# Gates and branch projections of a hybrid layer moved to token order, 512 columns wide, with the merged sum turned on TensorE

## The chip, the cores and the metric

One core of one Trainium2 chip. The metric is the device time of one execution in microseconds (us), the median of several runs. TensorE is called PE, VectorE DVE, ScalarE ACT, GpSimd POOL, SyncE SP.

## What is computed

Two blocks of two layers each, on 256 tokens of width 1024 in float32. Only a layer of the first block is touched:

```
x = x + 0.5 * swiglu(rms_norm(x, ffn1_norm), ...)
z = rms_norm(x, mix_norm) @ w_in                    # u, q, k, v (512 each), gl (2048)
y_pool = multiscale_pool(u, pool_w, pool_scale)     # [tokens, 512]
y_attn = moba_attention(rope(norm(q)), rope(norm(k)), v)
gates  = sigmoid(gl + b_gate).reshape(B, S, 2, D)
merged = gates[:, :, 0] * (y_pool @ w_branch_pool) + gates[:, :, 1] * (y_attn @ w_branch_attn)
x = x + merged @ w_out
x = x + 0.5 * swiglu(rms_norm(x, ffn2_norm), ...)
```

With 256 tokens in one block of keys the attention is causal softmax attention of 8 heads of 64. The second block has a mixer of its own (neighbourhood attention and retention, m = 0 to 41) that has token order already.

## The kernel before

Every product with a weight is made of three matmuls in a reduced float32 form (upper x lower, lower x upper, upper x upper parts; `product`, L1603 to L1606). The weights come as a stream of chunks of 128 x 2048 (1 MB) through SP's queue into three slots. For each chunk ACT makes the upper part (L562), DVE the lower part (L1007), PE uses both. Step m of an engine's program begins with a wait for PE to have finished chunk m (`chunk_done`), and ends with the split of the chunk that comes into the same slot, m + 3 (`split_after`). PE takes chunk m when its lower part is there (`take`).

There are two forms of product. `features` (L1643) holds 128 x 128 of the weights still and streams 256 tokens: the result has features on the partitions, two tiles of 256 columns in one PSUM bank, 48 matmuls for a chunk. `wide_tokens` (L1683) and `wide_whole` (L1700) hold 128 tokens of the activation still and stream 512 columns of weights: the result has tokens on the partitions, one bank for each half of the tokens (a = 0, 1), 24 matmuls for a chunk. `wide_tokens` takes the inner dimension in two chunks (part 0 and 1); it is used for v (m = 4, 5), for the output (m = 20 to 23) and in the second block.

The mixer of the first block runs over 24 chunks, m = 0 to 23: q and k (0 to 3), v (4, 5), u (6, 7), gate 0 (8 to 11), gate 1 (12 to 15), pool branch (16, 17), attention branch (18, 19), output (20 to 23). The order of every engine is written out by hand, step by step:

- PE, L1895 to L1964. Gate chunks 8 to 15 go by `features` to bank 4 or 5 by the parity of m; before chunk m PE waits for `mix_scaled` m - 7, the evacuation of chunk m - 2. Behind the chunk of a step come the pool product (m = 10), the weighing of the values (`weigh_values`, L1832, even m from 10), the transposes of the softmax weights (`turn_weights`, L1816, m = 8 to 15) and the scores (L1801, odd m from 7 to 13). The branches go by `features` to banks 0, 1 (m = 16), 2, 3 (17), 4, 5 (18) and 2, 3 (19). The product with the output weights wants the merged sum with features on the partitions, in upper and lower parts; chunks 20 and 21 wait for these (`merged_lo`).
- DVE, L1208 to L1290. Step m: wait for chunk m; evacuate the bank of a gate (times the norm's factors of the tokens, L1233, m = 6 to 15); the maxima of the scores of head m - 7 (L1149, L1157); the lower part of an attention pair (L1022, even m); the softmax weights (L1168), which wait for ACT's exponentials; the split (L1007), which waits for ACT's. At m = 16 and 17 the gate is multiplied by the pool branch; at m = 18 come four rounds of multiply and add for the attention branch and the lower parts of the sum (L1268 to L1286).
- ACT, L733 to L813. Step m: copies of turned weights (L679), exponentials (L660), the upper part of the split (L562), and at m = 15 and 16 the sigmoids of a gate, 8 instructions of 256 columns with the bias as a column (L803). At m = 18 the upper parts of the sum (L689).
- POOL, L473 to L504, the reciprocal roots of the heads' norms (L475) and the pool branch's sums (L481 to L503), which start when u has been evacuated (m = 7).

The second block turns its merged sum already: `turn_merged` (L1983) transposes tiles of 128 x 128 on PE into banks 6 and 7, ACT takes upper parts from there (L851), DVE lower ones.

## Time and profile before

| | |
|---|---|
| median of 3 runs | 1969.69 us (1969.32 to 1970.82) |
| the profiled execution | 1969.46 us |
| its span, first to last instruction | 1967.6 us |
| PE busy | 1955.9 us, 99% |
| DVE, ACT, POOL busy | 1363.1, 1029.6, 160.4 us |
| mean granted clock of PE | 0.999 of full speed |
| HBM | 182 GB/s over the span |
| chain that ended last | PE 98%, DVE 1%, ACT 1% |

Matmuls overlap: a busy time counts each from its start to its modelled end, so the price of a stretch of PE is read from the start of its first instruction to the start of the next one behind it. In the timeline a row is: start, duration, engine, line, operation, output and inputs, array and shape, count, and in brackets the idle time before it and what ended it. PE, DVE and ACT work at the same time; idle time of DVE or ACT costs something only where PE then waits.

### The profile page before, as it was taken

What the parts mean: (1) busy time and instruction counts of PE and PEld (TensorE: products, weight loads), DVE (VectorE), ACT (ScalarE), POOL (GpSimd) and SP (SyncE); (2) the same over time, 40 slices, a digit from 0 to 9 for tenths busy, and PEclk for the clock granted to TensorE, in tenths of its full rate; (3) what the DMA queues carried; (4) which work ended last, traced back from release to release, by engine and by line L of the source; (5) the groups of instructions that cost most, each with busy time, mean ns of one, the idle gap of its engine ahead of it and who ended that gap; (6) DMA issues with size and microseconds to landing.
All of it is one profiled execution on the core that took longest, in us unless ns stands there. A gap on an engine that the chain in (4) does not pass through costs nothing.

```text
span 1967.6 us, 28691 instructions
## 1 busy us (share of the span) xinstructions
PE 1955.9 (99%) x11078; PEld 1691.2 (86%) x11078; DVE 1363.1 (69%) x1660; ACT 1029.6 (52%) x1209; POOL 160.4 (8%) x148
## 2 busy tenths in 40 slices
PE   9999999999999999999999999999999999999998
PEld 8888999888888889998888978888888978888887
DVE  7666577666676666667666566577888666677887
ACT  6444545544454454565444553456556554456564
POOL 0000130000000003103001201040001301000000
PEclk9999999999999999999999999999999999999999
DMA  8555544555455545446555544564553554555552
GB/s 326 192 185 178 185 154 176 175 189 192 171 193 192 184 161 190 150 173 230 190 192 174 185 167 143 209 246 176 192 192 137 199 179 158 207 211 189 180 188 86
DMA packets 54689, 363.75 MB, mean 185 GB/s; under 512 B 6480, under 2 KB 7888, under 8 KB 11728
## 3 DMA queue, kind: packets, MB, share of 16 engines
q1 hardware_dynamic: 49680, 350.01, 49.7%
q0 software_dynamic: 1024, 7.34, 1.0%
q10 hardware_dynamic: 3904, 5.25, 0.9%
q8 instruction: 59, 0.97, 0.2%
q14 instruction: 22, 0.18, 0.0%
HBM read 357.33 MB, written 1.05 MB: 182 GB/s over the span
## 4 chain that ended last, share of the span: by engine, by line
PE 98%; DVE 1%; ACT 1%; DMA 0%; issue 0%; ACTq 0%; SPq 0%; DVEq 0%
PE gate_two L1674 13%; PE up_two L1674 12%; PE bank L1604 9%; PE bank L1606 9%; PE bank L1605 9%; PE gate_two L1604 8%; PE gate_two L1606 8%; PE gate_two L1605 8%; PE gate_two L1676 6%; PE up_two L1676 6%; PE bank L1801 1%; PE up_two L1832 1%; PE up_two L1816 1%; PE bank L2098 1%; PE gate_two L1616 0%; PE gate_two L1617 0%
## 5 line engine op out<-in xcount | busy, mean ns | idle before, releaser
L1007 DVE TENSOR_TENSOR w_lo<-raw,w_hi 128x2048 fp32r<-128x2048 f32 x318 | 734.8, 2312 | 255.9 <-ACT w_hi L562 255.9
L562 ACT ACTIVATE w_hi<-raw 128x2048 fp32r<-128x2048 f32 x322 | 614.3, 1908 | 85.6 <-PE bank L1606 60.0
L1674 PE MATMUL gate_two<-br_parts,w_hi 128*128 128x512 f32 x1056 | 376.4, 399 | 0.4 <-DVE w_lo L1194 0.4
L1674 PE MATMUL up_two<-br_parts,w_hi 128*128 128x512 f32 x1024 | 364.1, 398 | 0.0
L1676 PE MATMUL gate_two<-br_parts,w_lo 128*128 128x256 f32 x1056 | 296.2, 281 | 0.0
L1676 PE MATMUL up_two<-br_parts,w_lo 128*128 128x256 f32 x1024 | 287.4, 281 | 0.0
L1674 PEld LDWEIGHTS gate_two<-br_parts,w_hi 128*128 128x128 f32 x1056 | 198.4, 188 | 49.2 <-issue 1.2
L1674 PEld LDWEIGHTS up_two<-br_parts,w_hi 128*128 128x128 f32 x1024 | 192.4, 188 | 47.8
L1676 PEld LDWEIGHTS gate_two<-br_parts,w_lo 128*128 128x128 f32 x1056 | 199.4, 189 | 2.3
L1604 PE MATMUL gate_two<-br_parts,w_hi 128*128 128x256 f32 x672 | 193.3, 288 | 0.3 <-DVE w_lo L1007 0.3
L1676 PEld LDWEIGHTS up_two<-br_parts,w_lo 128*128 128x128 f32 x1024 | 193.3, 189 | 0.0
L1605 PE MATMUL gate_two<-br_parts,w_lo 128*128 128x256 f32 x672 | 190.0, 283 | 0.0
L1606 PE MATMUL gate_two<-br_parts,w_hi 128*128 128x256 f32 x672 | 190.0, 283 | 0.0
L1604 PE MATMUL bank<-w_lo,hid_hi 128*128 128x512 f32 x480 | 188.6, 393 | 0.0
L1606 PE MATMUL bank<-w_hi,hid_hi 128*128 128x512 f32 x480 | 187.7, 391 | 0.0
L1605 PE MATMUL bank<-w_hi,hid_lo 128*128 128x512 f32 x480 | 187.2, 390 | 0.0
L1604 PEld LDWEIGHTS gate_two<-br_parts,w_hi 128*128 128x128 f32 x672 | 128.7, 191 | 4.8 <-issue 4.4
L619 ACT ACTIVATE hid_hi<-area 128x512 fp32r<-128x512 f32 x60 | 37.9, 632 | 178.1 <-PE bank L1606 108.7
L1605 PEld LDWEIGHTS gate_two<-br_parts,w_lo 128*128 128x128 f32 x672 | 128.8, 192 | 0.0
L1606 PEld LDWEIGHTS gate_two<-br_parts,w_hi 128*128 128x128 f32 x672 | 128.7, 192 | 0.0
L1604 PE MATMUL gate_two<-w_lo,br_parts 128*128 128x512 f32 x320 | 128.0, 400 | 0.0
L1606 PE MATMUL gate_two<-w_hi,br_parts 128*128 128x512 f32 x320 | 125.0, 391 | 0.0
(283 smaller groups left out, 2954.3 us busy)
## 6 DMA issues: line engine op xcount, KB each, us to landing
raw<-stream SPq DMA_DIRECT2D x328, 1024.0 KB, 4.8
area<-rpb POOLq DMA_DIRECT2D x2, 1536.0 KB, 8.7
area<-rows POOLq DMA_DIRECT2D x3, 1024.0 KB, 5.3
raw<-stream SPq DMA_DIRECT2D x8, 256.0 KB, 7.1
softT<-area ACTq DMA_DIRECT2D x32, 64.0 KB, 4.9
konst<-consts SPq DMA_DIRECT2D x1, 1344.0 KB, 8.6
area<-xT ACTq DMA_DIRECT2D x4, 256.0 KB, 6.7
x<-x_rows SPq DMA_DIRECT2D x1, 1024.0 KB, 11.0
```

Source lines behind the costliest of these rows:

```text
L562: act.activation(w_hi[:, s, :], raw[:, s, :], ACT.Copy).then_inc(hi_ready[s], 1)
L619: act.activation(place[:, 0:2, :], hidden, ACT.Copy).then_inc(hid_hi_ready.sem, 1)
L1007: dve.tensor_tensor(w_lo[:, s, :], raw[:, s, :], w_hi[:, s, :].bitcast(F32), ALU.subtract).then_inc(lo_ready[s], 1)
L1604: pe.matmul(out, whi, xlo, start=start, stop=False, skip_group_check=True)
L1605: pe.matmul(out, wlo, xhi, start=False, stop=False, skip_group_check=True)
L1606: return pe.matmul(out, whi, xhi, start=False, stop=stop, skip_group_check=True)
L1674: pe.matmul(pair[:, f, :, :], w_hi[:, s, at:at + P], parts[:, :, k, :], start=k == 0, stop=False, skip_group_check=True)
L1676: e = pe.matmul(pair[:, f, 0, :], w_lo[:, s, at:at + P], parts[:, 0, k, :], start=False, stop=k == DT - 1, skip_group_check=True)
L1801: e = pe.matmul(banks[2 + half][:, a, 0:keys[a]], qk[rows, j, a * P:(a + 1) * P], qk[rows, HALVES + j, 0:keys[a]], start=True, stop=True, ...
L1816: e = pe.transpose(turned[:, at:at + P], soft[:, h % 2, a, k * P:(k + 1) * P], ident)
L1832: e = pe.matmul(banks[7][rows, j % 2, T - n:T], v_tok[:, k, h * HEAD_DIM:(h + 1) * HEAD_DIM], flat(softT[:, half, :, :])[:, at:at + n], st ...
L2098: e = pe.matmul(banks[h % 2][:, a, :], softT[:, h % 2, k, a * P:(a + 1) * P], ret_v[:, k, h * RET_V:(h + 1) * RET_V], start=k == 0, stop=k ...
```

## The change

- Gate chunks 8 to 15 are in token order and 512 columns wide (`wide_tokens`), a pair of chunks for 512 of the 2048 gate features: m = 8, 9 first half of gate 0, and so on. Each pair fills bank 4 (tokens 0 to 127) and bank 5 (tokens 128 to 255). A new signal `wide_half` tells that bank 4 is complete, in the middle of the second chunk. PE waits for the evacuation of bank 4 before m = 10, 12, 14, and for that of bank 5 before the second half of these chunks.
- DVE evacuates in steps 9, 11, 13, 15, twice each (`gated`): bank 4 at the head of the step, ahead of the wait for the chunk, bank 5 behind that wait. One operation multiplies by the norm's column and adds the bias, which is now a row: 1 MB a layer (128 equal rows of 2048), loaded through POOL's queue to `area3`, whose slots take the second gate later.
- ACT's sigmoids have no bias any more and are 2 instructions of 1024 columns per gate instead of 8.
- The branch chunks 16 to 19 go by `wide_whole`, in token order. DVE multiplies and adds for the attention branch in steps 18 and 19 (`second_branch`), each at half of the chunk and at its end.
- The merged sum is transposed on PE: 8 transposes in the middle of chunk 19, 8 in the middle of chunk 20, to banks 6 and 7. ACT and DVE take the upper and lower parts from there in steps 19 and 20, ahead of their waits for the chunk; the rounds of DVE's step 18 are gone.
- The stream of weights has the chunks in the new order; `cols1` loses the gate bias. `turn_merged` becomes a helper for both blocks; the second block's work is the same.

```diff
-        gates1 = (area2, area3)
-        gates2_tok, merged2_tok = [area[:, :, :].rearrange("p f t -> p (f t)").rearrange("p (a n) -> p a n", a=TT)
+        gate_slots = area3[:, :, :].rearrange("p f t -> p (f t)").rearrange("p (n c) -> p n c", n=HALVES)
+        gates2_tok, merged_tok = [area[:, :, :].rearrange("p f t -> p (f t)").rearrange("p (a n) -> p a n", a=TT)
...
-        wide_half = signal("wide_half", 1, 9)
+        wide_half = signal("wide_half", 5, 9)
+        branch_half = signal("branch_half", 2)
+        gate_rows_in = sem("gate_rows_in")
...
+                pool.wait_ge(qk_ms.sem, here.at(qk_ms, 4))
+                pool.dma_start(flat(area3[:, :, :]), rows1[layer:layer + 1].rearrange("a p n -> (a p) n")
+                               ).then_inc(gate_rows_in, 16)
...
-            def merged_upper(here, merged, upper, j):
-                act.wait_ge(merged_ready.sem, here.at(merged_ready, j + 1))
-                act.activation(upper[:, 2 * j:2 * j + 2, :], merged[:, 2 * j:2 * j + 2, :], ACT.Copy
-                               ).then_inc(merged_hi.sem, 1)
+            def turned_upper(here, upper, j):
+                act.wait_ge(merged_turned.sem, here.at(merged_turned, j // 2 + 1))
+                act.activation(upper[:, 2 * j:2 * j + 2, :], banks[6 + j % 2][:, :, :], ACT.Copy).then_inc(merged_hi.sem, 1)
...
+                    if m in (19, 20):
+                        for j in (2 * m - 38, 2 * m - 37):
+                            turned_upper(here, in_hi, j)
...
-                        for f in range(DT):
-                            col = C_GATE + DT * (m - 15) + f
-                            e = act.activation(gates[:, f, :], gates[:, f, :], ACT.Sigmoid, bias=cur[:, col:col + 1])
+                        for half in range(2):
+                            part = gates[:, half * D:(half + 1) * D]
+                            e = act.activation(part, part, ACT.Sigmoid)
...
+                def gated(m, a):
+                    gate, half = divmod((m - 9) // 2, 2)
+                    out = gate_slots[:, 2 * half + a, :] if gate else merged_tok[:, a, half * 2 * T:(half + 1) * 2 * T]
+                    dve.scalar_tensor_tensor(out=out, in0=flat(banks[4 + a][:, :, :]), scalar=rs[:, a:a + 1],
+                                             in1=gate_slots[:, (m - 9) // 2, :], op0=ALU.mult, op1=ALU.add
+                                             ).then_inc(mix_scaled.sem, 1)
+                def second_branch(h, a):
+                    part, out = gate_slots[:, 2 * h + a, :], merged_tok[:, a, h * 2 * T:(h + 1) * 2 * T]
+                    dve.tensor_tensor(part, part, flat(banks[(4, 2)[h] + a][:, :, :]), ALU.mult).then_inc(part_ready.sem, 1)
+                    dve.wait_ge(part_ready.sem, here.at(part_ready, 2 * h + a + 1))
+                    dve.tensor_tensor(out, out, part, ALU.add).then_inc(merged_ready.sem, 1)
                 for m in range(MIX1):
                     c = FFN_CHUNKS + m
                     if m == 0:
                         split_lo(2, here.uses(FFN_CHUNKS + 2))
+                    if m in (9, 11, 13, 15):
+                        dve.wait_ge(gate_rows_in, (layer + 1) * 16)
+                        dve.wait_ge(wide_half.sem, here.at(wide_half, (m - 5) // 2))
+                        gated(m, 0)
+                    if m in (18, 19):
+                        dve.wait_ge(branch_half.sem, here.at(branch_half, m - 17))
+                        if m == 18:
+                            dve.wait_ge(sig_ready.sem, here.at(sig_ready, 2))
+                            dve.wait_ge(branch_evac.sem, here.at(branch_evac, 2))
+                        second_branch(m - 18, 0)
+                    if m in (19, 20):
+                        for j in (2 * m - 38, 2 * m - 37):
+                            turned_lower(here, in_hi, in_lo, j)
...
-                    if 6 <= m < 16:
-                        branch, j = (m - 8) // HALVES, (m - 8) % HALVES
-                        out = u[:, 2 * (m - 6):2 * (m - 5), :] if m < 8 else gates1[branch][:, 2 * j:2 * j + 2, :]
-                        dve.tensor_tensor(out, banks[4 + m % 2][:, :, :], factors, ALU.mult).then_inc(mix_scaled.sem, 1)
+                    if m in (6, 7):
+                        dve.tensor_tensor(u[:, 2 * (m - 6):2 * (m - 5), :], banks[4 + m % 2][:, :, :], factors, ALU.mult
+                                          ).then_inc(mix_scaled.sem, 1)
+                    if m in (9, 11, 13, 15):
+                        gated(m, 1)
+                    if m in (18, 19):
+                        second_branch(m - 18, 1)
...
-                        for a in range(2):
-                            f = 4 * (m - 16) + 2 * a
-                            part = merged1[:, f:f + 2, :]
-                            e = dve.tensor_tensor(part, part, banks[f // 2][:, :, :], ALU.mult)
+                        for a in range(TT):
+                            part = merged_tok[:, a, (m - 16) * 2 * T:(m - 15) * 2 * T]
+                            e = dve.tensor_tensor(part, part, flat(banks[2 * m - 32 + a][:, :, :]), ALU.mult)
...
-                    if m == 18:
-                        dve.wait_ge(sig_ready.sem, here.at(sig_ready, 2))
-                        dve.wait_ge(branch_evac.sem, here.at(branch_evac, 2))
-                        for j in range(HALVES):
-                            f = 2 * j
-                            if j == 2:
-                                dve.wait_ge(attn_pair.sem, here.at(attn_pair, 1))
-                            elif j == 3:
-                                chunk_done(here, c + 1)
-                            part = gates1[1][:, f:f + 2, :]
-                            dve.tensor_tensor(part, part, banks[(4, 5, 2, 3)[j]][:, :, :], ALU.mult
-                                              ).then_inc(part_ready.sem, 1)
-                            dve.wait_ge(part_ready.sem, here.at(part_ready, j + 1))
-                            dve.tensor_tensor(merged1[:, f:f + 2, :], merged1[:, f:f + 2, :], part, ALU.add
-                                              ).then_inc(merged_ready.sem, 1)
-                            if j >= 1:
-                                merged_lower(here, j - 1, merged1, in_hi, in_lo)
-                        merged_lower(here, HALVES - 1, merged1, in_hi, in_lo)
...
+            def turn_merged(here, h, ready):
+                pe.wait_ge(merged_ready.sem, here.at(merged_ready, ready))
+                if h:
+                    pe.wait_ge(merged_lo.sem, here.at(merged_lo, 2))
+                for k in range(4 * h, 4 * h + 4):
+                    for a in range(TT):
+                        e = pe.transpose(turned_m[k][:, a * P:(a + 1) * P], merged_tok[:, a, k * P:(k + 1) * P], ident)
+                e.then_inc(merged_turned.sem, 1)
...
+                    elif 8 <= m < 16:
+                        wide_tokens(c, m % 2, (banks[4], banks[5]), br_hi, br_lo, wide_half,
+                                    before_second=lambda: pe.wait_ge(mix_scaled.sem, here.at(mix_scaled, m - 6)))
...
-                        outs = two(banks[at]) + two(banks[at + 1])
-                        hi, lo = (in_hi, in_lo) if m < 18 else (att_hi, att_lo)
-                        features(c, outs, hi, lo, HALVES, tile_done=second_half if m == 19 else None)
+                        if m < 18:
+                            wide_whole(c, banks[at:at + 2], in_hi, in_lo)
+                        else:
+                            wide_whole(c, banks[at:at + 2], att_hi, att_lo, branch_half,
+                                       before_second=(lambda: turn_merged(here, 0, 2)) if m == 19 else None)
...
+                                    before_second=(lambda: turn_merged(here, 1, 4)) if m == 20 else None,
...
-        chunks += _columns(w, 4, 512) + _wide(w, 1536) + _columns(w, 2) + _columns(w, 8, 2048)
+        chunks += _columns(w, 4, 512) + _wide(w, 1536) + _columns(w, 2)
+        for i in range(4):
+            chunks += _wide(w, 2048 + i * wide)
...
+        "rows1": np.stack([np.tile(a["b_gate"][l][None, :], (P, 1)) for l in range(DEPTH)]),
```

## Rows read from the trace of the kernel before

**Rows 1.** The page's table of engines: busy us, share of the span, instructions.

```profile
PE 1955.9 (99%) x11078; PEld 1691.2 (86%) x11078; DVE 1363.1 (69%) x1660; ACT 1029.6 (52%) x1209; POOL 160.4 (8%) x148
```

**Rows 2.** Table of waits, PE: us in total, times, longest us.

```profile
PE bank L1980 <- ACT x L833: 3.2, 2, 1.7
```

**Rows 3.** Busy time by stretch, whole core: gate chunks, branch chunks, the end.

```profile
core 0: us, PE busy (x) PEld busy (x) DVE busy (x) ACT busy (x) POOL busy (x), PEclk, DMA share, GB/s
249.00:305.37 56.37, 56.37 (x466) 53.17 (x465) 39.06 (x95) 29.17 (x54) 15.99 (x19) 1.00 0.43 150
305.37:329.46 24.09, 24.09 (x204) 23.64 (x202) 15.74 (x18) 17.49 (x26) 0.00 (x0) 1.00 0.51 175
1956.00:1960.00 4.00, 2.50 (x16) 1.72 (x15) 3.34 (x9) 1.52 (x2) 0.95 (x2) 1.00 0.00 0
1962.00:1965.00 3.00, 0.00 (x0) 0.00 (x0) 1.44 (x4) 1.46 (x4) 0.00 (x0) 0.98 0.56 201
1965.00:1967.60 2.60, 0.00 (x0) 0.00 (x0) 0.00 (x0) 0.00 (x0) 0.00 (x0) 0.50 0.53 171
```

**Rows 4.** Timeline of PE: first mixer, layers 1 and 2; last two, second block.

```profile
255.10 0.36 PE L1604 MATMUL gate_two<-br_parts,w_hi 128*128 128x256 f32 x1
...
260.93 0.49 PE L1816 MATMUL up_two<-konst,soft 128*128 128x128 f32 x3
...
262.20 0.39 PE L1604 MATMUL gate_two<-br_parts,w_hi 128*128 128x256 f32 x1
...
268.05 1.89 PE L1955 MATMUL bank<-area 128*128 128x256 f32 x8
...
270.98 0.36 PE L1604 MATMUL gate_two<-br_parts,w_hi 128*128 128x256 f32 x1
...
317.94 0.28 PE L1604 MATMUL gate_two<-att_lo,w_hi 128*128 128x256 f32 x1
...
323.70 0.28 PE L1604 MATMUL bank<-att_lo,w_hi 128*128 128x256 f32 x1
...
329.46 0.40 PE L1604 MATMUL bank<-w_lo,in_parts 128*128 128x512 f32 x1
...
345.84 1.03 PE L1730 MATMUL up_two<-konst,x 128*128 128x128 f32 x8
...
346.63 0.48 PE L1604 MATMUL bank<-w_lo,in_parts 128*128 128x512 f32 x1
...
790.49 0.49 PE L1816 MATMUL up_two<-konst,soft 128*128 128x128 f32 x3
...
1147.13 0.50 PE L1604 MATMUL gate_two<-w_lo,br_parts 128*128 128x512 f32 x1
...
1152.82 1.08 PE L1832 MATMUL up_two<-softT,area 128*64 128x256 f32 x8
```

**Rows 5.** Timeline of DVE, the same mixers: evacuations, and what follows the first.

```profile
263.81 0.68 DVE L1233 TENSOR_TENSOR area<-gate_two,factor 128x512 f32<-128x512 f32 x1
...
264.42 0.28 DVE L1149 CUSTOM_DVE_ANT_0 soft<-bank,konst 128x128 f32<-128x128 f32 x1
...
270.50 0.68 DVE L1233 TENSOR_TENSOR area<-gate_two,factor 128x512 f32<-128x512 f32 x1
...
277.35 0.68 DVE L1233 TENSOR_TENSOR area<-gate_two,factor 128x512 f32<-128x512 f32 x1
...
792.92 0.68 DVE L1233 TENSOR_TENSOR area<-gate_two,factor 128x512 f32<-128x512 f32 x1
```

**Rows 6.** Groups by form, DVE and ACT: busy us, mean ns, idle before.

```profile
L1007 DVE TENSOR_TENSOR w_lo<-raw,w_hi 128x2048 fp32r<-128x2048 f32 x318 | 734.8, 2312 | 255.9 <-ACT w_hi L562 255.9
...
L1397 DVE SCALAR_TENSOR_TENSOR softT<-bank,area 128x512 f32<-128x512 f32 x8 | 5.5, 692 | 12.1 <-PE bank L2088 12.1
...
L562 ACT ACTIVATE w_hi<-raw 128x2048 fp32r<-128x2048 f32 x322 | 614.3, 1908 | 85.6 <-PE bank L1606 60.0 <-PE gate_two L1606 18.3 <-DVE area L1184 3.7
```

**Rows 7.** The page's DMA issues: count, KB each, us to landing.

```profile
area<-rows POOLq DMA_DIRECT2D x3, 1024.0 KB, 5.3
```

More of the change, by code:

```diff
@@ L66 @@
 SMALL = 5 + len(WINDOWS)
[L69 to L70 removed]
+C_FFN1, C_MIX, C_FFN2, C_SCALE, C_Q, C_K = 0, 8, 16, 24, 28, 29
+COLS1 = 30
 FT = 2 * D_FF // P
@@ L124, in ffn_walk, with hybrid_and_neighbourhood_kernel @@
     step("D", PAIRS - 1, c0 + FFN_CHUNKS - 1, 0)
-def hybrid_and_neighbourhood_kernel(nc, xT, x_rows, stream, cols1, cols2, rows2, pool_w, pT, rpb, consts, out):
+def hybrid_and_neighbourhood_kernel(nc, xT, x_rows, stream, cols1, cols2, rows1, rows2, pool_w, pT, rpb, consts, out):
     ctx = ExitStack()
@@ L1054, in norm_factor, with turned_lower @@
                 dve.wait_ge(factor_ready.sem, here.at(factor_ready, n + 1))
-            def merged_lower(here, j, merged, upper, lower):
+            def turned_lower(here, upper, lower, j):
                 dve.wait_ge(merged_hi.sem, here.at(merged_hi, j + 1))
-                rest(lower[:, 2 * j:2 * j + 2, :], merged[:, 2 * j:2 * j + 2, :], upper[:, 2 * j:2 * j + 2, :]
+                rest(lower[:, 2 * j:2 * j + 2, :], banks[6 + j % 2][:, :, :], upper[:, 2 * j:2 * j + 2, :]
                      ).then_inc(merged_lo.sem, 1)
@@ L1451, in _ @@
                         for j in (m - 30, m - 29):
-                            dve.wait_ge(merged_hi.sem, here.at(merged_hi, j + 1))
-                            rest(br_lo[:, 2 * j:2 * j + 2, :], banks[6 + j % 2][:, :, :], br_hi[:, 2 * j:2 * j + 2, :]
-                                 ).then_inc(merged_lo.sem, 1)
+                            turned_lower(here, br_hi, br_lo, j)
                     if layer and 24 <= m < 28:
@@ L1698, in wide_tokens, with wide_whole @@
                 return e.then_inc(w_used[s], 1)
-            def wide_whole(c, pair, hi, lo):
+            def wide_whole(c, pair, hi, lo, half=None, before_second=None):
                 s = c % SLOTS
@@ L1704, in wide_whole @@
                     rows = slice(a * P, (a + 1) * P)
+                    if a == 1 and before_second:
+                        before_second()
                     for k in range(HALVES):
@@ L1708, in wide_whole @@
                                     w_lo[:, s, cols], start=k == 0, stop=k == HALVES - 1)
+                    if a == 0 and half:
+                        e.then_inc(half.sem, 1)
                 return e.then_inc(w_used[s], 1)
@@ L1981, in turn_normed @@
                         e.then_inc(z_turned.sem, 1)
-                def turn_merged(h):
-                    pe.wait_ge(merged_ready.sem, here.at(merged_ready, h + 1))
-                    if h:
-                        pe.wait_ge(merged_lo.sem, here.at(merged_lo, 2))
-                    for k in range(4 * h, 4 * h + 4):
-                        for a in range(TT):
-                            e = pe.transpose(turned_m[k][:, a * P:(a + 1) * P], merged2_tok[:, a, k * P:(k + 1) * P], ident)
-                    e.then_inc(merged_turned.sem, 1)
                 def ple_tokens(c, pair, between):
```

41 lines of the change are left out of this document (13 added, 28 removed).

## The prediction

> **What bounds the kernel now.** I read the page's table of engines first. TensorE (PE) is busy for 1955.9 of 1967.6 us and VectorE (DVE) for 1363.1 [rows 1], so time is won or lost only where PE's own work shrinks or where PE is made to wait. Then the table of waits: PE's longest is 1.7 us, twice, in front of a transpose of the second block [rows 2]. Then the table of busy time by stretch: in the gate chunks of the first mixer (m = 8 to 15) PE is busy for 56.37 of 56.37 us, in the branch chunks (m = 16 to 19) for 24.09 of 24.09 [rows 3]. PE waits for nobody there, and DVE, busy for 39.06 of those 56.37 us, seems to have room. That share misleads, as the waits below show.
>
> "Busy" counts overlapping matmuls, so I price PE from one start to another in the timeline. Chunk m = 18, 48 matmuls of 256 columns, goes from 317.94 to 323.70: 0.120 us each. The three 512-wide chunks m = 20 to 22, 72 matmuls, go from 329.46 to 345.84: 0.2275 us each. Eight transposes: 345.84 to 346.63, 0.79 us [rows 4].
>
> **The change, part by part, for each layer.**
> *Gate chunks.* 48 matmuls of 256 columns become 24 of 512. Before: 255.10 to 260.93 and 262.20 to 268.05, so 5.83 and 5.85 us for a chunk [rows 4]; I take 5.85. After: 24 x 0.2275 = 5.46, and 0.09 for the restart (the first 512-wide matmul behind small ones at 346.63 shows 0.48 us, where one in a stream shows 0.40), 5.55; a 512-wide chunk amid the second block's attention took 5.69 (1147.13 to 1152.82) [rows 4]. I take 5.60. Eight chunks: -2.0 us, bounds -1.3 and -2.4.
> *Branch chunks.* Of the 24.09 us, about 0.80 is an attention product behind m = 16, so 23.29 is theirs. After: 96 matmuls x 0.2275 + 2 x 0.09 = 22.02. -1.27 us.
> *Turning the merged sum.* 16 transposes in two bursts inside m = 19 and m = 20: 2 x (0.79 + 0.09) = +1.76 us, all on PE's path.
> Without waits that is -1.5 us a layer, -3.0 in all.
>
> A rule of the Trainium skill speaks against even this. By the rows two matmuls of 256 columns cost 13 ns more than the one of 512 that replaces them (2 x 120 - 227). The Trainium skill (TensorE: Matmul & The Clock Gate, section Back-to-back issue gap) gives an isolated gap of columns / 2.4 + 2.5 ns. By it a removed matmul would save 2.5 ns, the 576 removed ones 1.4 us instead of the 6.5 above, and the sum would be an estimate of 5 us more. The trace disagrees at both widths (120 against 109, 227 against 216), so I go by the rows.
>
> *Evacuation, the part that costs.* Before, each gate chunk m fills its own bank (4 or 5), and chunk m needs only the evacuation of m - 2: DVE may lie almost a chunk behind. After, a pair of chunks fills both banks, and m = 10, 12, 14 may not start until DVE has evacuated bank 4, which it does at the head of its step m = 9, 11, 13, behind the split of the weights of step m - 1. How late DVE is can be read. m = 9 ended at 260.93 and DVE came to its evacuation at 263.81, 2.9 us behind; in layer 2 it was 790.49 and 792.92, 2.4 behind [rows 4, 5]. By m = 11 it had caught up: 276.81 (270.98 + 5.83) against 277.35.
> After the change DVE has no evacuation in step 8, worth 0.61 us (263.81 to 264.42) [rows 5], so it is there at 263.20. The operation reads a bank, a column and a row; the like of it took 0.69 us [rows 6]. With 0.07 for the signal, PE may start m = 10 at 263.95. PE would be ready at: two chunks each 0.25 us shorter, 260.43, plus the transposes and scores that follow m = 9 (260.93 to 262.20, 1.27) = 261.70 [rows 4]. **Wait of 2.2 us.** In layer 2: 792.31 + 0.75 = 793.06 against 789.99 + 1.27 = 791.26, **1.8 us**.
> *m = 12 and m = 14.* The wait shifts PE: m = 10 ends at 269.55 instead of 268.05. DVE's step 10 hangs on PE's pool product: its next evacuation came 9.30 us behind the end of m = 10 (268.05 to 277.35) [rows 4, 5], so again 278.85 for bank 4, ready at 279.60. PE: 269.55 + 2.93 (268.05 to 270.98) + 5.60 + 1.27 = 279.35. Wait 0.25. From there DVE and ScalarE (ACT) go round in 6.1 us a chunk without an evacuation (264.42 to 270.50) and each pair holds two: 13.4 us, against PE's 2 x 5.60 + about 2.4 of attention = 13.6. So DVE stays some 0.7 us behind m = 13 and the next wait is about 0.1. m = 16 waits for no gate. Together 0.35 us, bounds 0 and 1.5.
> *m = 19 and m = 20.* DVE must multiply and add for bank 4 and for bank 5, 1.33 us each (two vector operations of 0.69 that overlap a little [rows 6]); the second starts when m = 18 ends, and PE asks 2.7 us later: no wait. Then come the split of the weights (2.2 us), the multiply and add for bank 2, and the lower part of the turned sum. From the end of m = 18 that is 2.1 (ACT's upper part, 1.9 and a signal) + 2.2 (DVE's lower part) + 1.33 + 0.7 = 6.33 [rows 6], where m = 20 begins at 2.73 + 0.88 + 2.73 = 6.34. Wait 0.1, bounds 0 and 1.
> *Loads and bias.* 1 MB of bias rows per layer comes through POOL's queue; such a load landed 5.3 us after issue [rows 7]. It is issued in step 4 or 5, behind POOL's last power for the keys, and first needed in step 9, three chunks of 5.8 us later: nothing, as long as it lands within 17 us. POOL's next work waits for the evacuation of m = 7, so the issue delays nothing there. ACT's 16 sigmoid instructions become 4, on ACT where nobody on the path waits: nothing.
>
> Layer 1: -2.0 - 1.27 + 1.76 + 2.2 + 0.35 + 0.1 = +1.1. Layer 2: +0.7. Together **+1.8 to +1.9 us**. The profiled execution took 1969.46 us (span 1967.6), 0.2 under the median of the runs shown; the sum gives 1971.3.
>
> **Rivals.**
> *A. No waits.* DVE reaches bank 4 before PE wants it, because the order of its queue matters less than its 31% idle time. Then only PE's sum is left: 1969.46 - 3.0 = 1966.5; with the low bound of 5.55 us a chunk, 1965.7; with both layers' chunks as short as the pure 5.46, 1964.2. For: DVE's idle time. Against: it was 2.9 us late at just this chunk.
> *B. The round of DVE and ACT becomes the bound, slower than before.* Place: from m = 10 to m = 15, where a split waits for ACT, ACT for the softmax, and the softmax for the last split. Before, step 9 took DVE 6.7 us with its one evacuation and step 10 6.85 [rows 5]. If later steps take 0.2 to 0.3 more than my 6.7 on average, the lag grows and the waits before m = 12 and m = 14 are 1 us each, and m = 20 waits 0.7 because DVE reaches step 18 late: +2.2 us a layer on the forecast, 1971.3 + 4.4 = 1975.7; with half of it 1973.5. It decides once DVE's pair of steps is longer than PE's 13.6 us. For: the two are 0.2 us apart. Against: step 9 took 6.1 without its evacuation, beside POOL's work on the pool branch.
> *C. The clock.* A wait before m = 10 lets the granted clock fall to 1.2 GHz. The stretch 1956 to 1960, in which PE stands for 1.5 us, shows a granted clock of 1.00; 1962 to 1965, without a matmul, 0.98; only then comes 0.50 [rows 3]. A wait of 2.2 lies with the first two. Price: a chunk at half clock, 5.6 us a layer, 1982.
> *D. Width saves nothing:* a chunk of 24 wide matmuls takes what 48 narrow ones took. Then both layers lose the 3.3 us above: 1971.3 + 6.5 = 1977.8. Against: 5.46 per chunk at 329.46 to 345.84 [rows 4]. The rule of the Trainium skill cited above (the same page and section) leans this way.
>
> **Numbers.** A measurement of this kernel can tell about 0.2%, 3.9 us, from no change: faster is below 1965.8, slower above 1973.6. The forecast 0.70, A 0.13, B 0.12, C 0.03, D 0.02. The forecast with its bounds (-0.8 and +1.4 for the chunks in both layers, -1 and +2.5 for the smaller waits) lies in 1969 to 1974; A adds the side down to 1966. The range 1967.0 to 1974.5 leaves half of A and B's upper half, C and D out. Faster: a third of A and a rest for chunks cheaper than I think, 0.08. Slower: C, D, most of B, 0.15. Same: 0.77.
>
> **What would show it.** In the changed profile: m = 10 begins 1.8 to 2.2 us late, behind DVE's evacuation, once a layer, where PE had no wait; wide gate chunks 5.5 to 5.7 us; two bursts of eight transposes a layer, 0.8 us each; the stretch from m = 8 to m = 22 about 1 us longer in each layer; all else unchanged. The prediction is wrong if no wait stands before m = 10, or if those before m = 12, 14 or 20 are over 1 us.

## The result and the profile after

| | before | changed |
|---|---|---|
| median, us | 1969.5 (1969.3 to 1970.8, 8 runs) | 1975.3 (1972.8 to 1978.0, 8 runs) |
| ratio | | 1.003, 95% interval 1.0019 to 1.0041 |
| profiled execution, us | 1969.46, span 1967.6 | 1978.0, span 1975.9 |

Slower by 5.8 us. The forecast was 1971.3 with a range up to 1974.5, so the time lies outside the range, though the sign was right; it is also above 1973.6, from which the prediction counts as slower (chance 0.15). The single executions, within 1.6 us of each other before, are now 5.3 us apart. The engines' shares hardly moved (the page's first part, changed kernel):

```profile
PE 1956.4 (99%) x10534; PEld 1664.9 (84%) x10534; DVE 1365.3 (69%) x1660; ACT 1024.6 (52%) x1185; POOL 163.6 (8%) x150
```

PE shows as many busy microseconds as in [rows 1], with 544 matmuls fewer: the profile counts time in which it runs slower as busy. The table of waits of PE (us in total, times, longest) has two lines of the first mixers that were not there:

```profile
PE gate_two L1608 <- DVE area L1208: 6.3, 6, 2.5
...
PE up_two L1834 <- DVE soft L1163: 0.7, 2, 0.4
```

L1208 is the new evacuation of the gates. Its six waits are three a layer, before m = 10, 12 and 14. The timeline of PE shows those of layer 1, and what follows the first:

```profile
261.79 0.55 PE L1834 MATMUL up_two<-konst,soft 128*128 128x128 f32 x3 [0.42 <-DVE soft L1163]
...
265.73 0.47 PE L1608 MATMUL gate_two<-w_lo,br_parts 128*128 128x512 f32 x1 [2.54 <-DVE area L1208]
...
267.33 0.63 PE L1608 MATMUL gate_two<-w_lo,br_parts 128*128 128x512 f32 x1
...
268.19 0.63 PE L1610 MATMUL gate_two<-w_hi,br_parts 128*128 128x512 f32 x1
268.61 0.63 PE L1608 MATMUL gate_two<-w_lo,br_parts 128*128 128x512 f32 x1
...
272.92 1.89 PE L1975 MATMUL bank<-area 128*128 128x256 f32 x8
...
275.84 0.48 PE L1608 MATMUL gate_two<-w_lo,br_parts 128*128 128x512 f32 x1
...
281.38 0.49 PE L1834 MATMUL up_two<-konst,soft 128*128 128x128 f32 x3
...
283.12 0.47 PE L1608 MATMUL gate_two<-w_lo,br_parts 128*128 128x512 f32 x1 [0.39 <-DVE area L1208]
...
296.94 0.47 PE L1608 MATMUL gate_two<-w_lo,br_parts 128*128 128x512 f32 x1 [0.20 <-DVE area L1208]
```

Chunk m = 11 takes 5.54 us (275.84 to 281.38), as forecast. Chunk m = 10, the same work, takes 7.19 (265.73 to 272.92). Busy time by stretch tells why; the columns are those of [rows 3], and the number before the DMA share is the granted clock:

```profile
265.73:268.00 2.27, 2.27 (x8) 1.86 (x9) 1.83 (x7) 0.37 (x1) 1.85 (x3) 0.79 0.72 242
268.00:270.50 2.50, 2.50 (x7) 1.93 (x7) 0.72 (x3) 2.50 (x5) 0.00 (x0) 0.51 0.50 206
270.50:272.92 2.42, 2.42 (x13) 1.94 (x11) 2.28 (x1) 0.11 (x1) 0.00 (x0) 1.00 0.00 0
799.00:802.50 3.50, 3.50 (x9) 2.77 (x10) 2.19 (x9) 1.59 (x5) 1.85 (x3) 0.57 0.94 300
```

The granted clock goes to half (0.51, the 1.2 GHz level) inside the chunk behind the wait, and comes back within it: the 512-wide matmuls start 0.42 to 0.43 us apart there (268.19 and 268.61), where the prediction read 0.2275 in the kernel before. Layer 2 does the same at 799.00, behind a wait of again 2.54 us. Each time the chunk is 1.6 us longer than its neighbours. From m = 8 to the end of m = 22 layer 1 took 101.61 us (249.26 to 350.87) against 96.84 (249.00 to 345.84), layer 2 3.6 us more than before.

### The profile page after: what moved, and what is told of

It reads as the page before. It is cut to its first block, busy times and chain, and to the rows that moved or that the text cites. A ratio compares the mean times of both kernels' runs of the same rounds, so it can differ in the third digit from the quotient of the medians.

```text
span 1975.9 us, 27591 instructions
## 1 busy us (share of the span) xinstructions
PE 1956.4 (99%) x10534; PEld 1664.9 (84%) x10534; DVE 1365.3 (69%) x1660; ACT 1024.6 (52%) x1185; POOL 163.6 (8%) x150
## 4 chain that ended last, share of the span: by engine, by line
PE 93%; ACT 2%; DVE 2%; issue 1%; DMA 1%; SPq 0%; ACTq 0%; DVEq 0%
PE gate_two L1678 12%; PE up_two L1678 12%; PE bank L1608 9%; PE bank L1610 9%; PE bank L1609 9%; PE gate_two L1608 7%; PE gate_two L1610 7%; PE gate_two L1609 7%; PE gate_two L1680 6%; PE up_two L1680 6%; ACT w_hi L565 1%; PE up_two L1850 1%; PE bank L2108 1%; DMA softT<-area 1%; PE up_two L1834 1%
## 5 line engine op out<-in xcount | busy, mean ns | idle before, releaser
L1680 PE MATMUL gate_two<-br_parts,w_lo 128*128 128x256 f32 x1056 | 296.2, 281 | 0.0
L1678 PEld LDWEIGHTS gate_two<-br_parts,w_hi 128*128 128x128 f32 x1056 | 198.4, 188 | 50.2 <-issue 2.2
L1680 PEld LDWEIGHTS gate_two<-br_parts,w_lo 128*128 128x128 f32 x1056 | 199.4, 189 | 2.3
L1608 PE MATMUL gate_two<-w_lo,br_parts 128*128 128x512 f32 x448 | 180.7, 403 | 6.3 <-DVE area L1208 6.3
L1610 PE MATMUL gate_two<-w_hi,br_parts 128*128 128x512 f32 x448 | 176.1, 393 | 0.0
L1609 PE MATMUL gate_two<-w_hi,br_parts 128*128 128x512 f32 x448 | 175.7, 392 | 0.0
L1608 PE MATMUL gate_two<-br_parts,w_hi 128*128 128x256 f32 x416 | 119.4, 287 | 0.2 <-DVE w_lo L1002 0.2
L1610 PE MATMUL gate_two<-br_parts,w_hi 128*128 128x256 f32 x416 | 117.7, 283 | 0.0
L1609 PE MATMUL gate_two<-br_parts,w_lo 128*128 128x256 f32 x416 | 117.6, 283 | 0.0
L617 ACT ACTIVATE area<-gate_two 128x512 f32<-128x512 f32 x66 | 39.4, 597 | 142.4 <-PE gate_two L1680 142.4
L617 ACT ACTIVATE area<-up_two 128x512 f32<-128x512 f32 x64 | 38.4, 600 | 134.9 <-PE up_two L1680 134.9
```

What stands on the lines that cost most here:

```text
L617: return act.activation(out, pair[:, :, 1, :], ACT.Copy)
L1608: pe.matmul(out, whi, xlo, start=start, stop=False, skip_group_check=True)
L1609: pe.matmul(out, wlo, xhi, start=False, stop=False, skip_group_check=True)
L1610: return pe.matmul(out, whi, xhi, start=False, stop=stop, skip_group_check=True)
L1678: pe.matmul(pair[:, f, :, :], w_hi[:, s, at:at + P], parts[:, :, k, :], start=k == 0, stop=False, skip_group_check=True)
L1680: e = pe.matmul(pair[:, f, 0, :], w_lo[:, s, at:at + P], parts[:, 0, k, :], start=False, stop=k == DT - 1, skip_group_check=True)
```

## The experiments

Three things looked guilty in this one profile: the waits for a single pair of accumulators, the clock behind the longest of them, and the new 1 MB load. For the load spoke a wait in the timeline of DVE, changed kernel:

```profile
245.52 0.69 DVE L1175 TENSOR_TENSOR softT<-softT,konst 128x512 f32<-128x512 f32 x1 [1.51 <-DMA softT<-area]
...
262.43 2.49 DVE L1002 TENSOR_TENSOR w_lo<-raw,w_hi 128x2048 fp32r<-128x2048 f32 x1 [0.69 <-ACT w_hi L565]
264.85 1.40 DVE L1208 SCALAR_TENSOR_TENSOR area<-gate_two,rs,area 128x512 f32<-128x512 f32 x2
```

DVE waits 1.51 us for the swapped halves of q and k, and reaches the gates at 264.85, 3 us behind the end of m = 9 (261.79). The experiments took each suspect alone.

### 1. Two pairs of accumulators

```diff
-                    dve.scalar_tensor_tensor(out=out, in0=flat(banks[4 + a][:, :, :]), scalar=rs[:, a:a + 1],
+                    dve.scalar_tensor_tensor(out=out, in0=flat(banks[(m - 1) // 2 % 2 * 4 + a][:, :, :]), scalar=rs[:, a:a + 1],
...
-                    elif 8 <= m < 16:
-                        pe.wait_ge(mix_scaled.sem, here.at(mix_scaled, m - 7))
...
+                    elif m == 10:
+                        pe.wait_ge(mix_scaled.sem, here.at(mix_scaled, 2))
...
-                        wide_tokens(c, m % 2, (banks[4], banks[5]), br_hi, br_lo, wide_half,
-                                    before_second=lambda: pe.wait_ge(mix_scaled.sem, here.at(mix_scaled, m - 6)))
+                        at = m // 2 % 2 * 4
+                        wide_tokens(c, m % 2, (banks[at], banks[at + 1]), br_hi, br_lo, wide_half)
...
                     if m == 10:
+                        pe.wait_ge(mix_scaled.sem, here.at(mix_scaled, 4))
```

The last line is needed since the pooling product behind m = 10 writes banks 0 and 1. Before m = 8, 12, 14 and 16 PE waits for the last reader of the pair that comes next.

> The edit: the four gate products take turns on two pairs of accumulators (0/1, 4/5, 0/1, 4/5) in place of one pair, so no gate chunk waits for VectorE to read the one before it. Theory (the wait before chunk m=10, 2.54 us, those before m=12 and m=14, 0.39 and 0.20, and the half clock that follows the first, 1.6 us, each once a layer, are what the change costs): all of these go, 4.7 us a layer, and the median falls from 1975.3 to about 1966, faster than the kernel before by 3 us. Rival (the bias-row load, or a longer TensorE path, is the cost and the wait only shows it): no more than the two longest waits go, the time stays at 1970 or above, and the pause comes back elsewhere (pooling products, m=12). Rival (the half clock comes from something else in the stretch, not from the pause): the clock still falls near chunk m=10, and the median stays above 1968.

1967.3 us (1966.8 to 1968.1, 11 runs), ratio to before 0.9987 (0.9978 to 0.9996). Its table of waits has no line for the gates any more, and the two stretches of layer 1 by busy time (gates, then branches to the end of m = 22) are:

```profile
249.67:303.84 54.17, 54.17 (x274) 42.70 (x273) 38.08 (x94) 29.57 (x54) 15.97 (x19) 1.00 0.45 156
303.84:345.20 41.36, 41.34 (x196) 33.57 (x195) 29.91 (x30) 21.43 (x18) 0.00 (x0) 1.00 0.50 178
```

So the waits and the clock behind them are all that makes the change slow; without them it is 2.2 us faster than before. The median was expected at about 1966 and is 1.3 above: the 4.7 us a layer were read from an execution of 1978.0 us, in which both layers lost the clock, and were taken off the median of 1975.3.

### 2 and 4. The load

```diff
@@ 2: in the changed kernel, on POOL
-    pool.wait_ge(qk_ms.sem, here.at(qk_ms, 4))
-    pool.dma_start(flat(area3[:, :, :]), rows1[layer:layer + 1]...)
     pool.wait_ge(mix_scaled.sem, here.at(mix_scaled, 2))
+    pool.dma_start(flat(area3[:, :, :]), rows1[layer:layer + 1]...)
@@ 4: the kernel before, with the load (and DVE waiting for it at m = 12)
+    pool.wait_ge(qk_ms.sem, here.at(qk_ms, 4))
+    pool.dma_start(flat(area3[:, :, :]), rows1[layer:layer + 1]...)
```

> The edit: GpSimd issues the 1 MB load of the bias rows after its wait for the pooling input (chunk m=7) instead of before it (chunk m=4), so it is off the DMA engines when the swapped halves of q and k travel. Theory: in layer 1 VectorE's evacuation of m=7 is no longer late (it starts within 0.7 us of TensorE's end, not 1.9), the waits of 0.32 and 0.42 us before the transposes of the weights go, the wait before m=10 falls by 0.3 us, and the half clock stays; the median falls by about 1 us to 1974.4. Rival (the load is the root of everything): the wait before m=10 falls under 1 us, the clock holds, and the median is under 1971. Rival (the load costs nothing, as forecast): 1975.3, and VectorE is late at m=7 all the same.

> The edit: the kernel before, with nothing of the change but the load of 1 MB of bias rows a layer, at the place where the changed kernel has it; nothing reads the rows. Prediction as recorded (the load costs nothing): 1969.5. Theory now: in layer 1 the swapped halves land about 1 us later and VectorE starts its evacuation of m=7 late by about 1.7 us, which the kernel before has room for (its next wait on VectorE is a chunk away): 1969.5 to 1970.3. If the load alone costs over 1.5 us, it is a large part of the loss of 5.8 us.

In experiment 4 nothing reads the rows; the edit also has DVE wait for them at m = 12. The later load of experiment 2 gave 1976.3 us (1973.8 to 1978.1, 8 runs), no gain where 1 us was expected. The kernel before with the load gave 1969.5 (11 runs), ratio 0.9999 (0.9990 to 1.0008), and there DVE's wait for the swapped halves in layer 1 was 0.41 us, with the load where the changed kernel has it. The kernel before, without the load, has 0.55, and the eight other profiled executions with the load in that place (experiments 1, 3, 5 to 9 and 11) have at most 0.86. The 1.51 us was one execution's: my reading of the single profile falls. In the run with the late load DVE waited 0.75 us, and the clock fell all the same (timeline of PE):

```profile
264.99 0.47 PE L1607 MATMUL gate_two<-w_lo,br_parts 128*128 128x512 f32 x1 [2.31 <-DVE area L1207]
...
272.12 1.89 PE L1974 MATMUL bank<-area 128*128 128x256 f32 x8
...
797.86 0.47 PE L1607 MATMUL gate_two<-w_lo,br_parts 128*128 128x512 f32 x1 [2.17 <-DVE area L1207]
...
804.99 1.89 PE L1974 MATMUL bank<-area 128*128 128x256 f32 x8
```

7.13 us a chunk both times. The two waits are within 0.1 and 0.4 us of the forecast ones, 2.2 and 1.8.

### 3 and 9. Work in place of the idle time

```diff
+    if m == 10:
+        for _ in range(22):      # 11 in experiment 9
+            pe.transpose(banks[0][:, 0, 0:P], ident, ident)
     take(here, c)
```

> The edit: 22 transposes of the identity into accumulator 0, about 2.2 us of work whose result nobody reads, stand on TensorE ahead of its wait before chunk m=10, and fill most of the pause of 2.54 us. The wait for VectorE is as before. Theory (the clock falls because TensorE stood still): the granted clock stays full through m=10, that chunk takes 5.6 us and not 7.2, and the median falls by 3.2 us (2 x 1.6), to about 1972.1, with a spread under 2 us in place of 5. Rival (the clock falls for another reason, such as the load of the chip as a whole in this stretch): m=10 still takes about 7.2 us and the median stays near 1975.3. Rival (the busy filler delays the chain): more than 2.5 us between the scores and m=10.

> The edit: the changed kernel with 11 transposes of the identity ahead of the wait before m=10 where the experiment with no idle time had 22, so 1.2 us of the pause of 2.2 to 2.5 us are filled and 1.0 to 1.3 us stay empty. Theory (the length of the pause decides: the kernel before stood still for 1.5 us with its clock kept, pauses of 2.2 to 2.5 us lose it in most executions): the clock holds, m=10 takes 5.6 us in both layers, and the median is that with 22 transposes, 1973.2, spread under 2 us. Rival (any pause in this stretch loses it): near 1975.3 to 1976.3.

With 22: 1973.2 us (1972.8 to 1975.4, 11 runs), 2.2 under the changed kernel. Expected was a gain of 3.2 and a spread under 2 us; but 3.2 supposed that every layer of every execution had lost the clock. With 11: 1973.6, near the expected 1973.2 (1972.9 to 1974.9, 11 runs), ratio to before 1.0019 (1.0010 to 1.0028). The timeline of PE, layer 1, with 22 and then with 11:

```profile
262.15 2.62 PE L1914 MATMUL bank<-konst 128*128 128x128 f32 x22
264.53 0.47 PE L1608 MATMUL gate_two<-w_lo,br_parts 128*128 128x512 f32 x1
...
270.10 1.89 PE L1978 MATMUL bank<-area 128*128 128x256 f32 x8
```

```profile
262.20 1.42 PE L1914 MATMUL bank<-konst 128*128 128x128 f32 x11
264.80 0.47 PE L1608 MATMUL gate_two<-w_lo,br_parts 128*128 128x512 f32 x1 [1.19 <-DVE area L1208]
...
270.37 1.89 PE L1978 MATMUL bank<-area 128*128 128x256 f32 x8
```

m = 10 takes 5.57 us in both, in layer 2 5.54 and 5.56. The useless work lies where PE would stand, and the granted clock is 1.00 through all four of these chunks. With 11 transposes PE still stands for 1.19 us in each layer, and that did no harm.

### 5. DVE's order

```diff
-    if m in (9, 11, 13, 15):                 # head of the step, behind the split of step m - 1
-        dve.wait_ge(gate_rows_in, (layer + 1) * 16)
-        dve.wait_ge(wide_half.sem, here.at(wide_half, (m - 5) // 2))
-        gated(m, 0)
     ...
+    if m in (8, 10, 12, 14):                 # end of the step before, ahead of the split
+        dve.wait_ge(gate_rows_in, (layer + 1) * 16)
+        dve.wait_ge(wide_half.sem, here.at(wide_half, (m - 4) // 2))
+        gated(m + 1, 0)
     if 0 < m < MIX1 - 2:
         split_after(here, c)
```

> The edit: the changed kernel with one accumulator pair, but VectorE reads the first half of each gate pair (m=9, 11, 13, 15) one place earlier in its queue, ahead of the 2.3 us split of a weight chunk instead of behind it. Theory (the wait before m=10 is VectorE's lateness: its queue is at the split when TensorE finishes the first half): the read starts at about 261 us instead of 264, the three waits a layer go or stay under 0.2 us, no chunk runs at half clock, and the median is within 1 us of the kernel with two pairs (1967.3). Rival (VectorE has no slack at all): the split moves back by 0.7 us, the next chunk waits for its low part, and the median stays above 1970.

1967.2 us (1967.0 to 1968.8, 11 runs), ratio to before 0.9990 (0.9981 to 0.9999). The first evacuation of each of the four pairs is moved. The timeline of DVE, layer 1:

```profile
260.38 0.74 DVE L1208 SCALAR_TENSOR_TENSOR area<-gate_two,rs,area 128x512 f32<-128x512 f32 x1
261.16 2.48 DVE L1002 TENSOR_TENSOR w_lo<-raw,w_hi 128x2048 fp32r<-128x2048 f32 x1
263.57 0.74 DVE L1208 SCALAR_TENSOR_TENSOR area<-gate_two,rs,area 128x512 f32<-128x512 f32 x1
```

Bank 4 is read before PE is done with the scores at 262.2, bank 5 is free at 264.3, just ahead of the second half of m = 10. No wait for the gates is left with one pair of accumulators. The wait was a matter of the place in DVE's queue, not of how much DVE has to do.

The profiled execution, at 1968.8 the slowest of the 11, shows one thing more. The kernel before has a pause of PE in the middle of the second block, the longest in [rows 2]; it kept the clock there. All 13 profiled executions of this document have it, with 1.66 to 1.72 us. In this one alone the clock fell behind it (timeline of PE for the kernel before and for this run, then busy time by stretch of this run):

```profile
1511.64 1.36 PE L1980 MATMUL bank<-konst,x 128*128 128x128 f32 x8 [1.72 <-ACT x L833]
```

```profile
1509.61 1.64 PE L2000 MATMUL bank<-konst,x 128*128 128x128 f32 x8 [1.70 <-ACT x L832]
```

```profile
1510.20:1513.60 3.40, 3.35 (x17) 3.28 (x17) 0.85 (x4) 0.88 (x2) 0.55 (x1) 0.55 0.00 0
```

### 6 and 10. The pause by itself

```diff
@@ 6: the kernel with two pairs
     elif m == 10:
-        pe.wait_ge(mix_scaled.sem, here.at(mix_scaled, 2))
+        pe.wait_ge(mix_scaled.sem, here.at(mix_scaled, 3))
@@ 10: the kernel before
-        pe.wait_ge(mix_scaled.sem, here.at(mix_scaled, m - 7))
+        pe.wait_ge(mix_scaled.sem, here.at(mix_scaled, 4 if m == 10 else m - 7))
```

> The edit: the kernel with two accumulator pairs, in which TensorE waits before m=10 for VectorE's read of the first half of the pair before (a wait that it doesn't need), and for nothing else new. Theory: the pause of 2.2 to 2.5 us is back once a layer and nothing else is; the granted clock falls within the chunk behind it in most executions, which costs up to 1.6 us more a layer; the median is 1967.3 + 4.5 to 1967.3 + 8, most likely 1973.5, and single runs spread by 2 us or more. Rival (the half clock belongs to something else that the second pair also took away): the clock holds and the median is 1971.8 to 1972.3 with a spread under 1.5 us. Rival (the pause is absorbed by later slack): under 1970.

> The edit: the kernel before, in which TensorE waits before m=10 for VectorE's read of m=9 where it needs that of m=8 alone; nothing of the change is in it. Theory (the pause and the clock behind it are costs by themselves, whatever the width of the columns): a pause of about 2.4 us once a layer, 4.8 us in all, and up to 3.2 us more where the clock falls behind it; the median lies between 1974.3 and 1977.5. Rival (the half clock needs the 512-column gates or the load of the bias rows): the clock holds, 1974.3 with a spread under 1.5 us. Rival (the pause is taken up by slack behind it): under 1972.

Experiment 6: 1976.1 us (1973.6 to 1976.4, 7 runs), above the expected 1971.8 to 1975.3. Two pauses of 2.44 us on average and two losses of 1.6 make 8.1, which gives 1975.4; four of the seven executions took 1976.1 to 1976.4. What the other 0.7 to 1.0 us are, no profile shows, since the profiled execution took 1973.6. Experiment 10: 1975.2 (1973.8 to 1976.9, 9 runs), ratio 1.0028 (1.0018 to 1.0038), within the expected range and with nothing of the change in it. One pause a layer, put into a kernel that runs at 1969.8 beside it, loses 5.4 us, of which the standing is 4.0 (2.08 + 1.92 in the profile). In each of the two profiled executions one layer kept its clock and the other lost it. The timeline of PE in experiment 6, then in experiment 10:

```profile
264.44 0.47 PE L1608 MATMUL gate_two<-w_lo,br_parts 128*128 128x512 f32 x1 [2.34 <-DVE area L1208]
...
269.97 1.89 PE L1982 MATMUL bank<-area 128*128 128x256 f32 x8
...
795.47 0.61 PE L1608 MATMUL gate_two<-w_lo,br_parts 128*128 128x512 f32 x1 [2.54 <-DVE area L1208]
...
802.61 1.89 PE L1982 MATMUL bank<-area 128*128 128x256 f32 x8
```

```profile
264.38 0.36 PE L1604 MATMUL gate_two<-br_parts,w_hi 128*128 128x256 f32 x1 [2.08 <-DVE area L1233]
...
271.69 1.89 PE L1955 MATMUL bank<-area 128*128 128x256 f32 x8
...
797.43 0.35 PE L1604 MATMUL gate_two<-br_parts,w_hi 128*128 128x256 f32 x1 [1.92 <-DVE area L1233]
...
803.25 1.89 PE L1955 MATMUL bank<-area 128*128 128x256 f32 x8
```

5.53 us behind the first pause of experiment 6, 7.14 behind the second; 7.31 and 5.82 in experiment 10, where the chunk has narrow columns.

### 7. Without the turning

```diff
-    for k in range(4 * h, 4 * h + 4):
-        for a in range(TT):
+    for k in range(4 * h, 4 * h + 1):
+        for a in range(1):
             e = pe.transpose(turned_m[k][:, a * P:(a + 1) * P], merged_tok[:, a, k * P:(k + 1) * P], ident)
```

> The edit: the kernel with two accumulator pairs, with 1 of 8 transposes left of each of the two bursts that turn the merged sum (the rest of the sum is not turned; the signals stay). Prediction's term for the turning: 16 transposes and two restarts, 1.76 us a layer. Expected: seven eighths of the transposes go, 1.4 us a layer, so 1967.3 - 2.8 = 1964.5. Rival (the transposes hide other waits: the splits of the turned sum come due at m=20): at m=20 a wait of 0.5 us or more opens and less than 2 us in all are gained.

1963.1 us (1962.8 to 1964.0, 6 runs), 4.2 under the kernel with two pairs, where 2.8 were expected. The reason is my edit: `turn_merged` serves the second block too, where it took out as many transposes again, which my expectation forgot. In the first block less was gained than expected: from m = 8 to the end of m = 22 layer 1 takes 94.80 us (249.57 to 344.37) in place of 95.53 (249.67 to 345.20), and layer 2 is 1.0 us shorter, 1.75 in both. The timeline of PE, layer 1:

```profile
324.00 0.27 PE L1740 MATMUL up_two<-konst,area 128*128 128x128 f32 x1
...
327.78 0.47 PE L1608 MATMUL bank<-w_lo,in_parts 128*128 128x512 f32 x1 [0.74 <-DVE in_parts L1017]
```

With one transpose left of the first burst PE arrives at m = 20 before the lower part of the turned sum is there; layer 2 waits 0.75. For the first block the rival holds (a wait over 0.5 us, a gain under 2). In layer 1 the seven eighths of the two bursts are worth 0.73 + 0.74 = 1.5 us, near the 1.54 of the prediction's term, but half of that hides a wait that stands there without them.

### 8. Narrow columns again

```diff
+def by_halves(out, whi, wlo, xhi, xlo, start, stop):
+    for f in range(2):
+        part = slice(f * T, (f + 1) * T)
+        e = product(out[:, part], whi, wlo, xhi[:, part], xlo[:, part], start and f == 0, stop)
+    return e
@@ wide_whole, and wide_tokens for m = 8 to 15
-    e = product(flat(pair[a][:, :, :]), ...)
+    e = by_halves(flat(pair[a][:, :, :]), ...)
```

> The edit: the kernel with two accumulator pairs, with every 512-column product of chunks m=8 to m=19 issued as two of 256 columns into the halves of the same accumulator. Prediction's term for the width: 2.0 us a layer in the gates and 1.27 in the branches, from the pitches 0.2275 and 2 x 0.120. Expected by it: 1967.3 + 6.5 = 1973.8, chunks of 5.85 instead of 5.57. Rival (recorded, width saves nothing): 1967.3. What the expectation leaves open is whether loading the same 128 x 128 weights twice costs anything.

1974.6 us (1974.1 to 1975.9, 8 runs), 7.3 over the kernel with two pairs. A gate chunk in the timeline of PE, from its first matmul to the transposes behind it:

```profile
255.28 0.36 PE L1608 MATMUL bank<-w_lo,br_parts 128*128 128x256 f32 x1
...
261.12 0.49 PE L1840 MATMUL up_two<-konst,soft 128*128 128x128 f32 x3
```

5.84 us, where the kernel with two pairs has 5.56. The eight gate chunks take 46.93 us in layer 1 instead of 44.71. `wide_whole` is shared with the second block: of the 6.9 us between the two profiled spans 5.9 lie in the first mixers, against the prediction's 6.5, and about 1 us elsewhere. The term was nearly right and the rival falls. By the formula of the Trainium skill for an isolated gap (TensorE: Matmul & The Clock Gate, section Back-to-back issue gap) the width would save 1.4 us in all, an estimate; the run does not agree with it for these products.

### 11. The changed kernel once more

> The changed kernel once more, beside the two others, for the spread of its single executions: between 1972.7 and 1978.1 us, with the granted clock of a whole execution (which counts how often the clock fell) lower in the slower ones. Where the clock fell in neither layer it should give 1973.0, in one 1974.6, in both 1976.2, by 1.6 us for each.

1975.7 us (1974.4 to 1977.0, 6 runs), ratio 1.0030. The times do not fall on three steps, as I had expected them to. In its profiled execution layer 1 lost the clock and layer 2 kept it, which should have given 1974.6; it took 1975.4. Timeline of PE, then busy time by stretch:

```profile
264.60 0.76 PE L1608 MATMUL gate_two<-w_lo,br_parts 128*128 128x512 f32 x1 [2.28 <-DVE area L1208]
...
271.53 1.89 PE L1975 MATMUL bank<-area 128*128 128x256 f32 x8
...
798.08 0.47 PE L1608 MATMUL gate_two<-w_lo,br_parts 128*128 128x512 f32 x1 [2.54 <-DVE area L1208]
...
803.63 1.89 PE L1975 MATMUL bank<-area 128*128 128x256 f32 x8
```

```profile
264.10:264.60 0.50, 0.00 (x0) 0.03 (x1) 0.50 (x2) 0.00 (x0) 0.50 (x2) 0.54 0.00 0
264.60:267.50 2.90, 2.90 (x7) 2.32 (x8) 1.84 (x7) 0.99 (x4) 1.85 (x3) 0.50 0.79 268
```

The longer pause, 2.54, is the one that kept it. In layer 1 the clock was down before PE had restarted. The half clock lasts as long as elsewhere, but some of it falls into the pause, and the chunk takes 6.93 us, 1.4 over its like and not 1.6.

## Why the prediction was wrong

The prediction had the right mechanism for the waits, and rightly forecast a small loss, but it left out a second loss that the longest wait brings with it. The medians split the distance between 1971.3 and 1975.3 into three parts. **The clock**, forecast at nothing, is about 2.2 us: 1975.3 against 1973.2 with the idle time filled. Seven losses in ten pauses, at 1.6 us, two pauses an execution, give the same 2.2. **The waits**, forecast at 4.9 us in both layers, are 5.9: 1973.2 with them, 1967.3 without. **PE's own sum**, forecast at 1966.5, is 1967.3, 0.8 more. Together 4.0.

*The clock (rival C, chance 0.03): the step that failed.* I wrote that a wait of 2.2 us "lies with the first two" stretches of [rows 3], a pause of 1.5 us with the clock kept and a longer one in which it hardly moved. That read the clock within and just behind a pause, at the end of the program, where little of PE's work was left. In the changed kernel the clock reads 1.00 through both pauses too, and falls only after PE has started again. The nearer row was PE's longest wait, 1.7 us in the middle of the second block [rows 2], which the prediction names in its first paragraph and leaves out of rival C. It kept the clock as well, but it is shorter than 2.2, so no row bore out a chance as low as 0.03. Of the ten pauses of 1.92 to 2.54 us before m = 10 in five profiled executions, seven were followed by half clock. The price was wrong as well: I put a whole chunk at half clock, 5.6 us, but half clock lasts some 3.4 us (about 267.0 to 270.4 in the changed kernel) and costs 1.4 to 1.6. With 1.6 us a layer C gives 1971.3 + 3.2 = 1974.5, within 1 us of the median measured.

*Waits.* The one before m = 10 had the right cause and nearly the right size: 2.17 to 2.54 us against 2.2 and 1.8. That layer 2 would wait 0.4 less, from one row of [rows 5], did not hold: in the four profiled executions with 512-wide gates (the changed kernel twice, experiments 2 and 6) it waited longer than layer 1 in two, as long in one and less in one. m = 12 waits 0.39 and m = 14 0.20, together 0.59 against 0.35, and no more: rival B, the round of DVE and ACT as the bound, did not come about. m = 20 begins 0.17 late (0.40 us behind the matmul before it at 333.10, in place of 0.23), forecast 0.1; the profile names no releaser for it. The waits of 0.32 and 0.42 us for the softmax in the changed profile are not regular: the same kernel in experiment 11 has none in layer 1 and one of 0.16 in layer 2, and no other profiled execution has any. They are part of why this execution, at 1978.0, is 2.7 us above its median.

*PE's sum.* With two pairs a wide gate chunk takes 5.54 to 5.69 us where I had 5.60, a burst of eight transposes 0.80 where I had 0.79 (changed kernel, 329.71 to 330.51):

```profile
329.71 1.04 PE L1740 MATMUL up_two<-konst,area 128*128 128x128 f32 x8
...
330.51 0.48 PE L1608 MATMUL bank<-w_lo,att_hi 128*128 128x512 f32 x1
```

Gate chunks: 56.37 us before [rows 3], 54.17 with two pairs, -2.2 against -2.0. Branch chunks and turning: 41.36 against 40.47 (305.37 to 345.84), +0.9 against +0.5. Beyond the four restarts of 0.09 that I had priced, the timeline with two pairs has m = 20 begin 0.18 late with a restart of 0.07, and 0.08 more ahead of the attention product. Layer 1 comes to -1.3, layer 2 to -1.1, where I had -1.5.

*Loads and bias: nothing.* Right for the load, by experiment 4; no wait for a sigmoid stands in the table of waits. *Rival D:* refuted by experiment 8. *Rival A* was no outcome of this change, but it is what experiments 1 and 5 make of it: 1967.3 and 1967.2.

*What stays open:* why one pause costs the clock and another of the same length, in the same place, does not (of the four pauses of 2.54 us one kept it, three lost it), and what sets the moment of the fall, which came from 0.5 us before PE's restart to 1.3 us behind it. No run varied the moment of a pause alone. Open too is what experiment 6 lost beyond its expected range.

## What to carry to other kernels

Where a change lets a pair of chunks share both accumulators, look at what stands ahead of the evacuation in the reader's queue, and not at how idle the reader is. Here moving the first evacuation of each pair ahead of a 2.3 us split gained 8.1 us (1975.3 to 1967.2), as much as a second pair of accumulators. And price a new pause on TensorE at its own length plus what the clock behind it may cost. One trace in which a pause kept the clock does not settle it: 1.7 us kept it 12 times and lost it once, 2.54 us kept it once and lost it three times.

The Trainium skill says the first in general (Perfetto Trace Analysis, section Matmuls): independent groups of matmuls should rotate through different banks, so that one is evacuated while the next is computed. Experiment 1 agrees, with 8.0 us. It says the second of another kernel (TensorE: Matmul & The Clock Gate, section A second HAM failure mode: psum-queue depth-cycling), where frequent short idle times between groups of matmuls make the clock go back and forth, at a cost in throughput. The windows of 0.51 and 0.57 above agree in part: here the pause is a single one a layer.

## What the hardware did that I had not expected

- A pause of 1.92 to 2.54 us in the middle of dense matmuls brought half clock 7 times in 10. Six times the fall came in the work behind it, up to 1.3 us after PE had started again (265.73 to about 267.0 in the changed kernel), once 0.5 us before that (experiment 11). The pause of 1.66 to 1.72 us in the second block brought it in 1 of 13 profiled executions, the pauses of 1.19 us in none of 2.
- The fall is short: full clock is back before the chunk ends, so it costs 1.4 to 1.6 us at 512 columns, and 1.5 at 256 (7.31 us against 5.82 in experiment 10).
- With transposes whose results nobody reads, 2.38 us of them in place of the pause, the clock read 1.00 in both layers of the profiled execution, the median fell by 2.2 us, and m = 10 began no later (264.53 us, against 264.60 to 265.73 without them).
